# The second kind's FFNs take x itself: transposes around the last projection tile, the root applied behind gate and up

## The reference

```
for l in range(DEPTH):                      # second kind
    h = rmsnorm(x, attn_norm[l])
    ...                                     # three mixers, gates, branches -> mixed
    x = x + mixed @ w_out[l]
    h = rmsnorm(x, ffn_norm[l])
    x = x + (jax.nn.silu(h @ w_ffn1[l]) * (h @ w_ffn3[l])) @ w_ffn2[l]
return rmsnorm(x, final_norm)
```

## Time and profile before

| | us |
|---|---|
| median of 3 runs | 2280.08 |
| the profiled execution, whole | 2280.72 |
| its span, first to last instruction | 2279.1 |
| PE matmul busy | 2217.8 (97%) |
| PE weight load busy | 1983.1 (87%) |
| DVE busy | 1625.4 (71%) |
| ACT busy | 1234.0 (54%) |
| bytes moved by DMA | 467.27 MB, 205 GB/s |

### The profile page before, as it was taken

One profiled execution on the slowest core, in us unless ns is written; L12 is line 12 of the kernel. 1 busy time (PEld: TensorE's weight loads), 2 busy tenths in 40 slices (PEclk: granted clock), 3 DMA queues, 4 the chain that ended last, 5 costly groups with the idle time before them and its releaser, 6 DMA issues.

```text
span 2279.1 us, 37401 instructions
## 1 busy us (share of the span) xinstructions
PE 2217.8 (97%) x14332; PEld 1983.1 (87%) x14332; DVE 1625.4 (71%) x2303; ACT 1234.0 (54%) x1721; POOL 77.0 (3%) x143
## 2 busy tenths in 40 slices
PE   3999999999999999999999999999999999999998
PEld 3888989988888888899988899889888998898887
DVE  7888777677778888777686667656656667566665
ACT  4445567564455446585554465655544556565444
POOL 0100000000000010000000000000000000000000
PEclk9999999999999999999999999999999999999999
DMA  8877564547666875655565546334555464344553
GB/s 344 311 277 266 190 229 163 194 178 282 242 236 244 298 272 189 229 181 199 194 222 193 191 160 212 130 142 157 199 187 189 157 234 139 131 165 176 198 189 111
DMA packets 79506, 467.27 MB, mean 205 GB/s; under 512 B 10080, under 2 KB 10800, under 8 KB 33168
## 3 DMA queue, kind: packets, MB, share of 16 engines
q1 hardware_dynamic: 58480, 389.38, 47.6%
q0 software_dynamic: 19312, 71.74, 8.8%
q10 hardware_dynamic: 1584, 4.36, 0.5%
HBM read 458.56 MB, written 1.05 MB: 202 GB/s over the span
## 4 chain that ended last, share of the span: by engine, by line
PE 90%; ACT 4%; DVE 2%; issue 1%; DMA 1%; ACTq 1%; DVEq 0%
PE ps L855 21%; PE ps L860 11%; PE ps L548 11%; PE ps L525 10%; PE ps L526 10%; PE ps L527 10%; PE ps L554 5%; PE ps L809 3%; PE ps L816 2%; PE ps L685 1%; PE ps L699 1%; PE ps L732 1%; DVE wlo L1815 1%; PE ps L651 1%; DMA raw<-in_ada 1%
## 5 line engine op out<-in xcount | busy, mean ns | idle before, releaser
L1815 DVE TENSOR_TENSOR wlo<-raw,whi 128x2048 fp32r<-128x2048 f32 x360 | 824.0, 2291 | 204.1 <-ACT whi L1231 190.8
L1231 ACT ACTIVATE whi<-raw 128x2048 fp32r<-128x2048 f32 x359 | 686.8, 1914 | 244.1 <-PE ps L527 195.5
L855 PE MATMUL ps<-hx,whi 128*128 128x512 f32 x2112 | 513.8, 391 | 0.1
L855 PEld LDWEIGHTS ps<-hx,whi 128*128 128x128 f32 x2112 | 392.0, 188 | 79.9 <-issue 0.6
L860 PE MATMUL ps<-hx,wlo 128*128 128x256 f32 x2112 | 288.5, 283 | 0.0
L860 PEld LDWEIGHTS ps<-hx,wlo 128*128 128x128 f32 x2112 | 276.8, 191 | 9.8
L548 PE MATMUL ps<-hx,whi 128*128 128x256 f32 x2176 | 276.6, 285 | 3.4 <-ACT set_a L1251 3.4
L548 PEld LDWEIGHTS ps<-hx,whi 128*128 128x128 f32 x2176 | 265.5, 191 | 6.7 <-issue 6.2
L525 PE MATMUL ps<-whi,yhi 128*128 128x512 f32 (+1 forms) x560 | 215.6, 385 | 0.0
L526 PE MATMUL ps<-wlo,yhi 128*128 128x512 f32 (+1 forms) x560 | 215.1, 384 | 0.0
L527 PE MATMUL ps<-whi,ylo 128*128 128x512 f32 (+1 forms) x560 | 214.4, 383 | 0.0
(11 more groups left out here) (281 smaller groups left out, 3002.6 us busy)
## 6 DMA issues: line engine op xcount, KB each, us to landing
raw<-in_w SPq DMA_DIRECT2D x360, 1024.0 KB, 4.9
adat<-in_ada POOLq DMA_DIRECT2D x128, 512.0 KB, 4.7
blk<-in_block POOLq DMA_DIRECT2D x2, 926.5 KB, 7.4
raw<-in_ada SPq DMA_DIRECT2D x3, 512.0 KB, 9.9
set_b<-in_ada SPq DMA_DIRECT2D x3, 512.0 KB, 11.6
raw<-in_ada ACTq DMA_DIRECT2D x3, 512.0 KB, 13.1
set_a<-set_b SPq DMA_DIRECT2D x24, 64.0 KB
x<-in_x POOLq DMA_DIRECT2D x1, 1024.0 KB, 10.2
```

What stands on the lines that cost most here:

```text
L855: mm(ps[:, bank + i, :].rearrange("p (a s) -> p a s", a=2), whi[:, slot, k * 256 + i * P:k * 256 + (i + 1) * P], hx[:, :, k, :], start=fir ...
L1231: A(whi[:, slot, :], raw[:, slot, :], ACT.Copy).then_inc(*T.counts("hi_ready"))
L1815: tt(wlo[:, slot, :], raw[:, slot, :], whi[:, slot, :].bitcast(F32), ALU.subtract)\
```

## The change

Four things. (1) In the second kind, the FFN's h is made of x without the root: `turn_x(0)` transposes side 0 of x between the two halves of the last projection tile, `turn_x(1)` side 1 after two of the eight blocks of the first gate tile; both go into the result banks themselves (`X_BANK`). ACT and DVE split these as before, with the gain. The roots are computed behind it, transposed from a column broadcast over 128 columns (`turn_roots`, between the first gate tile and the first up tile), copied to `root_row` by DVE (`take_roots`), and every chunk's gate sum and up sum is multiplied by it. The fillers of this end go. (2) The fillers of the other ends: 28 become 34 where there is a gate (first kind), with 5 more between the two token halves of `turn_rows`; 28 become 18 behind the second kind's FFN. (3) In the differential attention ACT takes token half 0 of `vg` ahead of `exps` of s = 2, and half 1 behind it. (4) The counts in `LAYER2` follow.

```diff
             def turn_rows(between=0):
                 for t in range(2):
...
+                    if t == 0:
+                        keep_busy(between, 2)
+            def turn_x(c_):                                             # PE
+                pe.wait_ge(*T.next("x_ready", 2))
+                for t in range(2):
+                    for m in range(4 * c_, 4 * c_ + 4):
+                        at = (m % 2) * S + t * P
+                        last = nc.tensor.transpose(ps[:, X_BANK[m // 2], at:at + P], x[:, t, m * P:(m + 1) * P], ident)
+                        if t and m % 2:
+                            last.then_inc(*T.counts("tr_ready"))
+            def turn_roots():
+                pe.wait_ge(*T.next("rx_ready", 2))
+                for t in range(2):
+                    last = nc.tensor.transpose(ps[:, 0, t * P:(t + 1) * P], r_x[:, t:t + 1].broadcast_to([P, P]), ident)
+                last.then_inc(*T.counts("row_ready"))
                 for c_ in range(2):                                     # output_projection
                     slot = tile()
                     rows(slot, 1, c_, 0).then_inc(*T.counts("bank_done"))
+                    if c_ and gate is None:
+                        turn_x(0)
                     rows(slot, 1, c_, 1).then_inc(*T.counts("tile_used"))
-                keep_busy(28 if gate is not None else 12, 7)
-                turn_rows()
+                if gate is None:
+                    return
+                keep_busy(34 if gate is not None else 17, 7)
+                turn_rows(between=5 if gate is not None else 0)
                 keep_busy(8, 2)
+            def features_of_x(bank):
+                slot = tile()
+                for k in range(KD):
+                    if k == 2:
+                        turn_x(1)
                     pe.wait_ge(*T.next("h_ready"))
...
             def gate_up(of_x=False):
...
+                    if of_x and fresh_h[0]:
+                        features_of_x(bank).then_inc(*T.counts("tile_used"))
+                        turn_roots()
+                        continue
...
-                keep_busy(28, 7)                                        # ffn
-                turn_rows()
+                keep_busy(34 if gate is not None else 18, 7)
+                turn_rows(between=5 if gate is not None else 0)
...
+            def pieces_of_x(c_, gain):                                  # ACT
+                for m in range(4 * c_, 4 * c_ + 4):
+                    if m % 2 == 0:
+                        act.wait_ge(*T.next("tr_ready"))
+                    A(hhi[:, m, :], ps[:, X_BANK[m // 2], m % 2 * S:(m % 2 + 1) * S], ACT.Copy, scale=gain[:, m:m + 1])\
+                        .then_inc(*T.counts("t2_ready"))
+            def output_projection_and_h(gain):
+                tile_done(False)
+                tile_done(False)
+                split_ahead()
+                T.n["bank_done"] += 2
+                x_square(0, 0)
+                T.n["tile_used"] += 1
+                split_ahead()
+                x_square(1, 0)
+                pieces_of_x(0, gain)
+                x_square(0, 1)
+                x_square(1, 1)
+                T.n["tile_used"] += 1
+                pieces_of_x(1, gain)
+                for t in range(2):
+                    row_root(x_sums, t, 2 + t, r_x, T.counts("rx_ready"))
...
                     exps(ins, s, t0)                                    # attend, with ahead(s) in front of it
...
-                            take_values(vg)                             # beside_diff, s == 2
+                            take_second(vg)
-                    t0, _ = attend(diff, 1, beside_diff)
+                    t0, _ = attend(diff, 1, beside_diff, lambda s: take_first(vg) if s == 2 else None)
...
+            def lows_of_x(pair, gain):                                  # DVE
+                v.wait_ge(*T.next("t2_ready", 2))
+                for m in (2 * pair, 2 * pair + 1):
+                    stt(out=hlo[:, m, :], in0=ps[:, X_BANK[m // 2], ...], scalar=gain[:, m:m + 1], ...)
+            def output_projection_and_h(gain):
+                tile_done(False)
+                tile_done(False)
+                split_low()
+                add_plain(0, 0, "bank_done")
+                add_plain(1, 0, "tile_used")
+                add_plain(0, 1, "bank_done")
+                lows_of_x(0, gain)
+                add_plain(1, 1, "tile_used", True)
+                for pair in range(1, 4):
+                    lows_of_x(pair, gain)
+                split_low()
+            def take_roots():                                           # ahead of the FFN's first gate_up
+                v.wait_ge(*T.next("row_ready"))
+                nc.vector.tensor_copy(root_row, ps[:, 0, 0:S])
+                v.drain()
...
-                    tt(gate_sum, gate_sum, ps[:, 4:6, 0:S], ALU.add).then_inc(*T.counts("ga_ready"))
+                    last = tt(gate_sum, gate_sum, ps[:, 4:6, 0:S], ALU.add)
+                    if plain:
+                        v.drain()
+                        last = tt(gate_sum, gate_sum, over(root_row, 2), ALU.mult)
+                    last.then_inc(*T.counts("ga_ready"))
...
                     tt(up_sum, up_sum, ps[:, 6:8, 0:S], ALU.add).then_inc(*T.counts("ua_ready"))
                     v.drain()
+                    if plain:
+                        tt(up_sum, up_sum, over(root_row, 2), ALU.mult)
+                        v.drain()
```

More of the change, by code:

```diff
@@ L122 @@
     "tile_used": 75, "ug_ready": 1, "vq_ready": 1, "vr_ready": 1, "vs_ready": 1, "vsum_ready": 1, "wt_ready":
[L123 to L128, removed]
+    1, "x_ready": 7, "xb32_ready": 2, "xb_ready": 2, "y_ready": 8, "yhi_ready": 4,
+    "xsq_ready": 1,
+    "x_rms": 2,
+    "u_ready": 3,
+    "u1_ready": 1,
+    "tr_ready": 8,
+    "rx_ready": 2,
+    "row_ready": 1}
 FFN_BODY = {"a_ready": 2, "g_chunks": 2, "gu_free": 2, "gb_ready": 2, "ga_ready": 2, "ub_ready": 2, "ua_ready": 2, "hi_ready": 6, "lo_ready": 6, "raw_full0": 2, "raw_full1": 2,
@@ L262, in build @@
         H_BANK = (6, 7, 0, 1)
+        X_BANK = (0, 2, 1, 3)
+        root_row = rstd[:, 0, :]
         ACROSS = ((0, 0), (1, 0), (0, 1), (1, 1))
@@ L641, in keep_busy, with turn_rows @@
                     mm(ps[:, bank, 0:S], idle[:, 0:P], idle[:, P:P + S], start=True, stop=True)
-            def turn_rows():
+            def turn_rows(between=0):
                 for t in range(2):
@@ L866, in features_fresh @@
                 for k in range(KD):
+                    pe.wait_ge(*T.next("h_ready"))
+                    for i in range(2):
+                        wide(bank, slot, k, i, k == 0)
+                        last = narrow(bank, slot, k, i, k == KD - 1)
+                fresh_h[0] = False
+                return last
+            def features_of_x(bank):
[3 more added lines that the diff above has]
+                        turn_x(1)
                     pe.wait_ge(*T.next("h_ready"))
@@ L885, in features_wide, with gate_up @@
                 return last
-            def gate_up():
+            def gate_up(of_x=False):
                 n = T.n["g_chunks"]
@@ L908, in down, with ffn @@
                 last.then_inc(*T.counts("tile_used"))
-            def ffn(gate=None, more=True):
-                gate_up()
+            def ffn(gate=None, more=True, of_x=False):
+                gate_up(of_x)
                 gate_up()
@@ L1215, in _ @@
                     fresh_h[0] = True
-                    ffn(more=layer < DEPTH - 1)
+                    ffn(more=layer < DEPTH - 1, of_x=True)
         @block.scalar
@@ L1377, in turned, with attend @@
                 A(bufC[:, u % 2, :], ps[:, bank, 0:384], ACT.Copy).then_inc(*T.counts("pt_ready"))
-            def attend(ins, n, beside):
+            def attend(ins, n, beside, ahead=lambda s: None):
                 t0, o0 = T.n["t_ready"], T.n["o_ready"]
@@ L1382, in attend @@
                     split_ahead()
+                    ahead(s)
                     exps(ins, s, t0)
@@ L1872, in add_result, with add_plain @@
                         last.then_inc(*T.counts("x_ready"))
-            def add_plain(t, c_, done):
+            def add_plain(t, c_, done, signal_last=False):
                 v.wait_ge(*T.next(done))
                 last = tt(x[:, t, side(c_)], x[:, t, side(c_)], ps[:, 2 * t + c_, :], ALU.add)
-                if (t, c_) != (1, 1):
+                if (t, c_) != (1, 1) or signal_last:
                     last.then_inc(*T.counts("x_ready"))
@@ L1946, in sublayer_begin @@
                 split_low()
+            def lows_of_x(pair, gain):
+                v.wait_ge(*T.next("t2_ready", 2))
+                for m in (2 * pair, 2 * pair + 1):
+                    stt(out=hlo[:, m, :], in0=ps[:, X_BANK[m // 2], m % 2 * S:(m % 2 + 1) * S],
+                        scalar=gain[:, m:m + 1], in1=hhi[:, m, :].bitcast(F32), op0=ALU.mult,
+                        op1=ALU.subtract).then_inc(*T.counts("h_ready"))
             def new_gain():
```

(4 more changed lines are left out.)

27 lines of the change are left out of this document (14 added, 13 removed).

## The result

The changed kernel takes 2268.74 us (median of 5 runs, 2268.52 to 2269.39), the kernel before in the same comparison 2280.12 (5 runs): ratio 0.9950, 95% interval 0.9939 to 0.9961. The forecast was 2269.7 with 2267.6 to 2273.4. The profiled execution took 2269.39 whole, its span is 2267.8 against 2279.1: 11.3 us less. The prediction's sum was 10.4.

The account below looks back on a forecast made before the run. PE was taken as the bound, busy 16.57 of 16.57 us per FFN chunk. Savings 6.0 + 1.0 + 3.4 = 10.4 us took the median 2280.08 to 2269.7; own range 2268.2 to 2271.8, with two rivals inside 2267.6 to 2273.4.

Parts of the forecast that it names:

- Part 1, x itself: Last projection tile to up tile, second kind: 10.87 us becomes 7.83, 3.0 saved, twice; put at 6.0.
- the wait at block 4: First gate tile: PE waits for block 4 of h, 0.15 us taken, bounds 0 and 1.
- The wait at block 2: First gate tile: side 1 of x is ready before PE's second transposes; no wait, 0.5 us to spare.
- some 5 us old: Inside the last projection tile: age of side 0's two additions when the first transposes need them, so no wait.
- Rival F: First 8 transposes find x late and stall inside the projection tile, up to 1 us each time: 2271.7; chance 0.03.
- C: h is late by 1.5 us, the first gate tile stalls at blocks 0 and 4: 2272.7; chance 0.07.
- The root: Every chunk: DVE's two multiplications, 1.56 us, stay beside PE; cost 0, 17.2 us if on the path in every chunk.
- The new wait at the head of DVE's queue: First gate tile: DVE waits for PE's root transposes; cost 0 with 0.9 us spare, bounds 0 and 1.5, twice.
- Part 2, fillers: Behind the second kind's FFN, 18 fillers for 28: 1.0 us saved once; 0 at the first kind's six ends.
- rival E: Without fillers PE's clock drops to 1.2 GHz for the gate tile, both times: 2281.2, no difference; chance 0.03.
- Part 3, the values: Differential attention: PE no longer waits for ACT's first copy of the values; 1.71 us, twice, 3.4.
- Rival B: Differential attention: PE waits for the gate tile's high or low part instead of the bank: 2273.1; chance 0.07.

Follow-up runs that it names:

- x4: The changed kernel with the first 8 transposes of x behind the last projection tile instead of inside it: 2272.13 us.
- x5: The changed kernel with the other 8 transposes ahead of block 4 of the first gate tile instead of block 2: 2271.62 us.
- x3: The changed kernel without DVE's two multiplications by the root in each chunk: 2268.25 us.
- x7: The changed kernel with the up sum multiplied by the root four times instead of once in every chunk of the second kind's FFNs: 2271.93 us.
- x2: The changed kernel with the old fillers at the ends, 28 and none between the token halves: 2270.05 us.
- x6: The changed kernel without any filler: 2276.43 us (11 runs).
- x1: The changed kernel with ACT taking both halves of the values behind exps again: 2272.89 us.
- x9: The changed kernel with PE not waiting for the last of ACT's copies ahead of the first kind's first attention: 2267.29 us.
- x10: The changed kernel with the second kind's gates by token multiplied behind the projection of the features instead of ahead of it: 2274.35 us.

## Why the prediction was right

**Part 1, x itself.** Predicted 3.04 us per place, measured 3.29. The early transposes took 0.79 (0.86 taken), with 0.10 more in the half tile behind them (1610.24 to 1613.06, 2.82, against 13.59 - 10.87 = 2.72), which the prediction had at nothing. From the gate tile to the up tile 6.69 (6.97 taken): transposes 0.79 for 0.86, roots 0.13 for 0.23, the wait at block 4 0.11 for 0.15, and the tile itself 5.66 for 5.73. Four small terms, all on the high side. The wait at block 2, put at nothing with 0.5 us to spare, had just that: x was there at 2077.85 + 0.69 = 2078.54, the transposes started at 2079.05. x4 and x5 show what the cover is worth: 3.4 and 2.9 us. One reading was too generous: the two additions that the first transposes need were to be "some 5 us old". The younger of the two (DVE, from 1606.93 for 0.69 us) ended 1.8 us ahead of 1609.45, and 1.8 us in layer 2 as well. It was still in time. Rival F would have shown idle time ahead of the transposes at 1609.45, C a wait of about 1.5 us for h; neither is there.

**The root.** Predicted 0 with 1.1 us of room in the tightest chunk. x3: nothing. x7: 0.9 us of room, as 1.42 of 2.30 added came through. The new wait at the head of DVE's queue cost nothing: the copy starts behind a low part without a gap. From the up tile on, the layers were 0.12 and 0.04 us longer. It is not the root: x3, without the multiplications, has 176.86 and 183.41, within 0.04 of the changed kernel. No row explains the 0.12, and it stays open.

**Part 2, fillers.** Predicted 1.0 behind the FFN, measured 0.99 by marks, and 0.99 back in x2. The six ends of the first kind: 0, measured 0.01 at the first (x2), though 9 us went from the list of waits. The granted clock was 1.00 from 1609.45 to 1619.75, with 18 transposes and no filler, so rival E did not come. x6 shows that the clock does fall in this kernel, to 0.50, at ends where PE is idle for up to 4.2 us. The Trainium skill, page "TensorE: Matmul & The Clock Gate", section "Part 4: PE-mode transpose", says that a transpose doesn't count as busy time of PE in the way of a matmul. Groups of eight between real matmuls, at 1.00, are in line with that as the prediction read it. So is x6's first end, where the clock stayed at 0.50 through all 16 transposes and rose behind the first matmuls of the tile, but no run here puts the transposes alone to the test.

**Part 3, the values.** The place and mechanism were right, the size was off: 1.71 was taken, 1.93 and 1.89 came by the marks (x1: 1.96). This is the term that was mis-sized: the prediction's "PE was free at 1501.98 - 1.71 = 1500.27" took the idle time of a row as the distance to the place where the tile could begin. That idle time counts from the modelled end of the transposes ahead of it. Start to start it was 1499.78 to 1501.98 = 2.20, and the gate tile now starts 0.24 behind the first of the three transposes: 1.96 saved. The Trainium skill, page "Perfetto Trace Analysis", section "Tensor Engine Instruction (MATMUL, LD_WEIGHTS)", says that TensorE's ends in a profile are computed and not observed. The runs are in line with it: 1.7 in the list of waits and 1.96 by the marks of x1, 1.2 and 1.5 in x5, 1.17 and 1.42 in x7. Rival B would have left a wait of PE for a high or low part there; the tile starts without one.

**Sum.** 6.0 + 1.0 + 3.4 = 10.4 against 6.6 + 1.0 + 3.8 = 11.4, less 0.2 in the FFNs and 0.1 at the start the other way: 11.3. The time fell within the own range, 1 us under the forecast: 0.4 us from the values' row and 0.6 from the two places of part 1, less the 0.2 and with the 0.1 above. No large errors cancelled here; each of the three parts came out within 0.6 us of its term.

## What to carry to other kernels

Where a wait of PE was taken away or made here by moving work, it was worth more than the idle time in brackets ahead of the matmul, by 0.25 us in x1, x5 and x7 and by under 0.1 in x9: take the distance between the two starts, less what the instructions between take when they run packed. Fillers are worth having (x6: 7.7 us without any), but more of them inside a wait that had 28 cost nothing and gained nothing; those that reached past the signal cost their length, so fit their number to the signal. Before an operation is moved past another on one engine, look at every engine that answers it: in x10 waits of 0.9 us were taken off PE, and 5.4 came back by way of ACT's queue.

## What was not expected of the hardware

- Without fillers the whole loss was 7.7 us where at least 21 were expected. The clock was back at 1.00 within the next tile (0.9 us behind its start at the first end, 3.3 at the third), and the first eight of the 16 slow transposes lay inside a wait for ACT that was there anyway.
- Inside a projection tile at clock 1.00, eight transposes of 128x128 float32 take 0.79 us from first start to the next matmul (0.099 each), and the first wide matmul behind them is followed 0.32 us later, where the pace is 0.23: a group costs 0.88.
